# Last modulation loads between the Toeplitz transfers, and the head norm's root on ScalarE

## What is computed

```python
cond = jax.nn.silu(c)
mod = cond @ ada_w[i] + ada_b[i]
h = modulate(rms_norm(x, norm_g[i, 0]), sh_t, sc_t)
...
# S5: diagonal state per group, chunked scan
y = y + d_skip * u32
z = jax.nn.gelu(y)
val, gate = jnp.split(z @ w_glu, 2, axis=-1)
...
# attention, per head and block of 128 queries
p = jax.nn.softmax(jnp.where(mask, s, -jnp.inf), axis=-1)
attn = p[:, :, 0] - lam * p[:, :, 1]
o = attn @ v
o = rms_norm(o, subln_g) * (1.0 - lambda_init)      # over the 128 channels of a head
return o.reshape(bsz, seq_len, d) @ w_o
```

## Time and profile before

| | |
|---|---|
| median of 3 runs | 1313.02 us (1311.71 to 1313.73) |
| the profiled execution | 1311.49 us |
| its span in the trace | 1309.7 us |
| PE busy | 1232.2 us, 94% |
| DVE, ACT, POOL busy | 59%, 39%, 30% |
| chain that ended last | PE 75%, DVE 10%, issue 3%, ACT 2% |

### The profile page before, as it was taken

One profiled execution on the slowest core, in us unless ns is written; L12 is line 12 of the kernel. 1 busy time (PEld: TensorE's weight loads), 2 busy tenths in 40 slices (PEclk: granted clock), 3 DMA queues, 4 the chain that ended last, 5 costly groups with the idle time before them and its releaser, 6 DMA issues.

```text
span 1309.7 us, 17877 instructions
## 1 busy us (share of the span) xinstructions
PE 1232.2 (94%) x6557; PEld 991.2 (76%) x6557; DVE 779.2 (59%) x1096; ACT 508.8 (39%) x780; POOL 393.4 (30%) x267
## 2 busy tenths in 40 slices
PE   4978999899999999999999989898999999999995
PEld 2756888688888887888787767576788888878883
DVE  8976687878954443253955687867754444442323
ACT  3373443243433443132332545445344444442311
POOL 4970100255634342000204343400243344440001
PEclk9988999899989999999999999999899999999997
DMA  7857645146732223231223313111032222223311
GB/s 298 353 161 205 256 165 213 58 165 218 299 136 96 78 99 112 97 127 67 77 97 97 97 50 96 49 65 65 33 102 95 97 97 97 98 97 120 111 51 64
DMA packets 26697, 162.21 MB, mean 124 GB/s; under 512 B 4496, under 2 KB 4816, under 8 KB 8400
## 3 DMA queue, kind: packets, MB, share of 16 engines
q1 hardware_dynamic: 25632, 161.15, 35.0%
q10 hardware_dynamic: 1008, 0.28, 0.1%
HBM read 152.76 MB, written 2.10 MB: 118 GB/s over the span
## 4 chain that ended last, share of the span: by engine, by line
PE 75%; DVE 10%; issue 3%; ACT 2%; POOL 0%; DVEq 0%; ACTq 0%
PE psum L1777 16%; PE psum L1779 16%; PE psum L1778 16%; PE psum L1900 6%; PE psum L1902 6%; PE psum L1901 6%; PE psum L1980 1%; PE psum L1955 1%; PE psum L1940 1%; PE psum L1942 1%; PE psum L1941 1%; DVE wlo L1206 1%; DVE stat L1486 1%; PE psum L1826 1%; DVE ssum L1300 1%
## 5 line engine op out<-in xcount | busy, mean ns | idle before, releaser
L1777 PE MATMUL psum<-hhi,whi 128*128 128x512 f32 x960 | 382.4, 398 | 2.3 <-DVE hlo L1349 1.4
L1779 PE MATMUL psum<-hhi,wlo 128*128 128x512 f32 x960 | 376.3, 392 | 0.0
L1778 PE MATMUL psum<-hlo,whi 128*128 128x512 f32 x960 | 376.2, 392 | 0.0
L1206 DVE TENSOR_TENSOR wlo<-raw,whi 128x2048 fp32r<-128x2048 f32 x81 | 192.4, 2375 | 177.2 <-ACT whi L702 177.2
L544 POOL TENSOR_TENSOR ca<-ca,cb 128x512 f32<-128x512 f32 x44 | 146.2, 3323 | 243.4 <-ACT ca L813 243.4
L702 ACT ACTIVATE whi<-raw 128x2048 fp32r<-128x2048 f32 x80 | 153.2, 1915 | 164.4 <-PE psum L1902 146.1
L1777 PEld LDWEIGHTS psum<-hhi,whi 128*128 128x128 f32 x960 | 181.7, 189 | 43.1 <-issue 2.4
L1779 PEld LDWEIGHTS psum<-hhi,wlo 128*128 128x128 f32 x960 | 181.5, 189 | 38.9
L1778 PEld LDWEIGHTS psum<-hlo,whi 128*128 128x128 f32 x960 | 181.9, 189 | 36.1
L1377 DVE SCALAR_TENSOR_TENSOR ca<-psum,convp,ca 128x511 f32<-128x511 f32 x44 | 33.0, 750 | 219.2 <-ACT ca L809 219.2
L1900 PE MATMUL psum<-ghi,whi 128*128 128x512 f32 x352 | 137.2, 390 | 1.5 <-DVE wlo L1206 1.5
(11 more groups left out here) (334 smaller groups left out, 1676.2 us busy)
## 6 DMA issues: line engine op xcount, KB each, us to landing
raw<-in_units SPq DMA_DIRECT2D x92, 1024.0 KB, 4.8
ada_raw<-in_ada_w SPq DMA_DIRECT2D x24, 1024.0 KB, 7.3
ada_ring<-in_ada_w SPq DMA_DIRECT2D x24, 1024.0 KB, 4.8
qk_sw<-ca SPq DMA_DIRECT2D x32, 128.0 KB, 2.3
u<-in_x_blocks SPq DMA_DIRECT2D x1, 2048.0 KB, 7.6
x<-in_x_t SPq DMA_DIRECT2D x1, 2048.0 KB, 8.5
out_t<-x SPq DMA_DIRECT2D x8, 256.0 KB, 2.0
bc_par<-in_s_bc SPq DMA_DIRECT2D x1, 1024.0 KB, 5.2
```

The source lines that it names most:

```text
L1206: TT(wlo[:, s, :], raw[:, s, :], whi[:, s, :].bitcast(F32), ALU.subtract).then_inc(split_lo, 1)
L1777: M(out, w_hi, hi[:, k, :], start=(k == 0), stop=False)
L1778: M(out, w_hi, lo[:, k, :], start=False, stop=False)
L1779: return M(out, w_lo, hi[:, k, :], start=False, stop=(k == KT - 1))
```

## The change

Three things move in the S5 stage. SP issues modulation loads 21 to 23 between the copies of Toeplitz piece 0 and those of piece 1. PE does `inputs(2)` after modulation unit 18 in place of 19, units 19 and 20 before `local(0)`, and `back(0)` before `local(1)`. ACT copies the second modulation row right after the scaling of piece 1, ahead of half of piece 2's scaling and of the copies of the kernel.

In attention DVE no longer makes the first guess. It signals the variance (`hn_arg`), ACT computes exp(-0.5 ln v) in `head_root` (`Ln`, then `Exp`, on 4 elements a partition) after `turned(a_, 0)` and ahead of the half split of the next weights, and DVE waits for it (`hn_root`) and does one Newton round in place of three. `HEAD_STEPS` counts DVE's linked operations, 5 in place of 13.

```diff
-            for piece in range(2):
-                load_toeplitz(piece)
+            load_toeplitz(0)
             for n in range(21, N_ADA_PE):
                 load_ada0(n)
+            load_toeplitz(1)
             sp.wait_ge(ada_used, N_ADA_PE)
...
             for quarter in range(4):
                 scaled(1, quarter)
+            copy_row(1)
             for quarter in range(2):
                 scaled(2, quarter)
...
-            copy_row(1)
...
+            def head_root(h):
+
+                ln, root = nwt[:, 0, 0:QT], nwt[:, 3, 0:QT]
+                act.wait_ge(hn_arg, h + 1)
+                A(ln, nwt[:, 2, 0:QT], ACT.Ln).then_inc(hn_root, 1)
+                act.wait_ge(hn_root, 2 * h + 1)
+                A(root, ln, ACT.Exp, scale=-0.5).then_inc(hn_root, 1)
...
                 turned(a_, 0)
+                if not first:
+                    head_root(a_ - 1)
...
             copy_output(HEADS - 1)
+            head_root(HEADS - 1)
...
-                lk(TS(t.bitcast(I32), v.bitcast(I32), 1, None, ALU.logical_shift_right))
-                lk(TS(d.bitcast(I32), t.bitcast(I32), -1.0, RSQRT_MAGIC, ALU.mult, ALU.add))
+                dve.sem_inc(hn_arg, 1)
                 yield
-                for i in range(3):
-                    lk(TT(t, d, d, ALU.mult))
-                    lk(STT(t, t, -0.5, v, ALU.mult, ALU.mult))
-                    lk(STT(d, t, 1.5, d, ALU.add, ALU.mult))
-                    if i == 0:
-                        yield
+                dve.wait_ge(hn_root, 2 * h + 2)
+                lk(TT(t, d, d, ALU.mult))
+                lk(STT(t, t, -0.5, v, ALU.mult, ALU.mult))
+                lk(STT(d, t, 1.5, d, ALU.add, ALU.mult))
+                yield
...
             inputs(1)
-            ada_units(16, 20)
+            ada_units(16, 19)
             inputs(2)
+            ada_units(19, 21)
             local(0)
             carried(0)
-            ada_units(20, N_ADA_PE)
+            ada_units(21, N_ADA_PE)
             inputs(3)
+            back(0)
             local(1)
-            back(0)
             carried(1)
```

More of the change, by code:

```diff
@@ L72 @@
 ROUND = 1.5 * 2.0 ** 23
-HEAD_STEPS = 13
+HEAD_STEPS = 5
 RSQRT_MAGIC = float(0x5F3759DF)
@@ L266, in build @@
         mask_ready = sem("mask_ready")
+        hn_arg, hn_root = sem("hn_arg"), sem("hn_root")
         att_step, smax, hn_step = sem("att_step"), sem("smax"), sem("hn_step")
```

## The result

The change takes 1303.69 us, median of five executions (1298.67 to 1304.31), against 1312.94 of the kernel before (1311.71 to 1313.73): ratio 0.9924, 95% interval 0.9905 to 0.9943. That is 9.2 us faster where 16.2 were forecast. The profiled execution took 1303.19 us.

A forecast was written before the change was run, and what follows sets the result against it. The prediction took PE as the bound, gaining only where it waits or runs at the low clock. S5's 6.1 us and attention's 10.1 made 16.2 less, 1295.3 profiled, 1296.8 as median, forecast 1297 us, range 1292 to 1305.

The forecast's parts named there:

- half of attention given back: Rival in attention: semaphore waits use ACT's 0.15 us slack, slow head keeps low clock; attention gives 5 us: 1302; chance 15%.
- both together: Rival: attention gives 5 us and S5, its transfers only reordered, 2.6 us: 1305.5; chance 4%.
- Steps 1 and 2: S5: second row copied early removes 0.72 us wait, worth 0 alone; units 19 and 20 (1.8 us) fill the 3.17 wait.
- Step 3 failed in its size: S5: loads 21 to 23 follow piece 0 on SP; unit 23 starts at 104.15 and ends at 105.1 us.
- Step 4 was right for piece 1: S5: piece 1, copied behind the loads at 131 GB/s, is off at 106.6 to 108.3; local(1) waits at most 0.5 us.
- Step 5 was the right chain: S5: weight units issued at 105.2 instead of 112.20; piece 2 lands at 116.8, 6.4 us earlier; PE waits 2 to 3.
- Step 7's half chance: S5: half a chance that the new wait brings the low clock to local(2), 1.4 us, so 0.7 counted.
- Step 2 held: Steady head: ACT's two loads, Ln and Exp take 2.98 us; exps(2) starts at 778.75; the 0.58 us wait goes.
- The rival in which ACT becomes the bound: Rival: ACT drains between functions, 2.98 us more a head; attention loses 10.4: 1317; chance 6%.
- Step 3 failed: Steady head: DVE's second softmax block 1.2 us earlier, later steps meet PE; 1.65 us in each of four heads: 6.6.
- Step 4: Head at 838 to 856 (second from end): att 2.8 us earlier, weigh 2.3, clock 1.2; together 3.5 us.
- Step 5: First head, last head and tail: ACT costs 0.3 and 0.2, earlier final att gives 0.8, cover just gone; together 0.

## Why the prediction was right or wrong

The sign was right, and 1303.7 lies in the range of 1292 to 1305, but not in the likeliest case (1293.5 to 1299.5). It lies between two rivals, half of attention given back (1302) and both together (1305.5). Attention came out near the first (4.2, where it had 5), but not by what that rival gave as its reason, ACT's slack: the agreement in time is luck. The range held because its upper end was set to take in each of the two halves; both parts of the sum were too large.

**S5.** Forecast 6.1 us; 2.6 at the first GEMM, 3.2 at attention, with 1.1 lost ahead of the stage, where the kernel products ended later, half of it behind an idle time of 2.02 us (1.47 before) that the trace puts down to issue. So the stage itself gave some 4. By the whole time, the S5 part alone gave 5.6.
- Steps 1 and 2 held: no wait for the row, and two units in 1.90 us inside the wait for piece 0, of which 1.57 are left.
- Step 3 failed in its size. Unit 23 was to start 9.85 us after piece 0 was off the engines, as it had after piece 1. It started at 106.01, 1.9 later than forecast: 1.1 of that because piece 0 itself was off the engines only at about 95.4 (94.3 before), and 0.75 because it came 10.6 us after that and not 9.85. The step took the loads as having the engines to themselves; piece 1's copies were issued 0.04 us behind them and ran beside them. The unit then took 1.88 us at the low clock, and not 0.9: the prediction had the low clock cost something only at `local(2)`, and this microsecond stands on the chain that releases the weight units.
- Step 4 was right for piece 1: it had left the engines by 107, and `local(1)` waited for nothing. But its 131 GB/s was no rate of the small copies. In windows of half a microsecond of before nothing moves from 100.0 to 100.5, and then 262 GB/s, which by the order of the queue is the first load. That 106.6 came out is luck in this term.
- Step 5 was the right chain. From the weight units' issue to piece 2 it took 11.5 us (107.95 to 119.47), against 11.0 before. The start was 2.75 us later than the 105.2 forecast (1.1 by piece 0, 0.75 by the loads, the rest by unit 23), and so was the piece (119.47 where 116.8 was forecast). The wait of 2.34 us is in the 2 to 3 forecast.
- Step 6 held, the 0.45 us wait is gone. Step 7's half chance went against it: 1.66 us of low clock in `local(2)`. It was a chance indeed: with the round moved the same place kept the high clock behind a longer wait.
- The experiments add which edit it was: SP's order alone gives all of it, PE's none. Steps 1 and 2, and the order of `back(0)`, are worth nothing that can be measured.

**Attention.** Forecast 10.1 us, got 4.2. The steady heads fell short (2.1 us of 6.6), and not the second head from the end (3.1 of 3.5).
- Step 1 held: no wait at the second block in the steady head.
- Step 2 held almost to the tenth, the tight place included: load, `Ln`, load, `Exp` in 2.98 us, half split 1.04, exponentials at once, and no wait of PE for them. The rival in which ACT becomes the bound was wrong. Without the loads the time is the same within the measurement.
- Step 3 failed: "DVE's second softmax block is still 1.2 us earlier than before". It was 0.16 earlier (9.65 us behind the second block's maximum, 9.81 before). The prediction kept the slow durations of two operations of the block, but let the half split and the round move to an earlier place at the durations of their old place. That place lies beside POOL's sums. The rows of before had held the warning: the two integer operations took 1.22 and 1.19 us for 4 elements where the fastest took 0.17. The prediction read this as a price of those operations, and took it to go with them. It is the price of the place, and goes to whatever stands there: the run without POOL's sums and the one with the round moved show it. With the round behind the fourth maximum the period came to 20.2 us, as the step had said (20.1).
- Step 4: the waits fell from 4.57 us (0.32, 2.98 and 1.27) to 2.16 (0.32, 0.52 and 1.32), and the granted clock rose from 0.81 to 0.91 in a stretch of 18 us. PE's wait for `att` is 2.46 us shorter, near the forecast, but the one for `att_t`, which was to come 2.3 us earlier, is as long as it was. The head took 3.1 us less all the same, clock included.
- Step 5: the final `att` did come earlier, but PE gained 0.26 us by it and not 0.8. The same turn waits for ACT's `cb` too, the copy of what PE turned just before, and that copy now comes last. Before, and after:

```profile
875.16 0.66 PE L1971 MATMUL psum<-ident,att 128*128 128x128 f32 x4 [1.13 <-DVE att L1501]
```

```profile
867.53 0.63 PE L1982 MATMUL psum<-ident,att 128*128 128x128 f32 x4 [0.87 <-ACT cb L873]
```

  The table loads have no part in it: ACT stood idle for 1.46 us ahead of `cb` in both kernels, waiting for PE. The two heads ahead of the steady ones together lost 0.7 us, where 0.3 was forecast for one of them. The tail came out as said, with the cover just gone: the norm's last step ends at 875.47 and PE's turn stands at 875.53.

The Trainium skill (SBUF — State Buffer, Who interferes with whom) states that a VectorE instruction with two inputs in SBUF contends with a GpSimd instruction that reads SBUF, that one in a 2-port mode contends with GpSimd as well, that the shared ports are an exclusive lock, and that the order of issue decides who blocks. The traces agree: 0.16 against 1.23 us for the same 4 elements. No run here shows the ports themselves. They also show the other side. POOL's sums over the run (ns, min/median/max):

```profile
L579 POOL TENSOR_TENSOR qk<-qk,qk_sw x16: 1263/1335/2272, 699.7 to 839.7; 128x512 f32<-128x512 f32 x16
```

One takes 1.26 us at least, and up to 2.27 in a pair that DVE's half split runs beside. In the steady head this can be read as turns, an estimate from these durations: POOL's first sum to about 777.0, DVE's half split (1.2 us of work) to 778.1, POOL's second to 779.23, and the round's first operation behind it, to 779.25.

The Trainium skill (ScalarE: Activation LUTs, What ACT_TABLE_LOAD costs) adds some 1380 ns of drain to every switch to another set. None of the 16 loads here shows it: in the rows above the next activation starts 0.02 us behind the load. The trace decides.

## What to carry to other kernels

When a tiny operation is slow in a trace and fast elsewhere, find what runs beside it before counting its time as saved: the next operation may inherit the place. On a queue of transfers, moving what releases the next issue forward was worth more here (6.1 us) than filling the wait in front of it (nothing measurable); but loads and small copies issued back to back run at once, so the last load landed some 0.75 us later than forecast for loads alone. A copy's rate is read from a window in which nothing else moves. And a gain in an early stage is only the program's once the places with a low clock further on have been read too.

## What the runs showed of the hardware

- A VectorE operation with two inputs of 4 elements a partition takes 0.16 us, and 1.2 where GpSimd sums 128x512 beside it; one such sum takes 1.26 us at least and up to 2.27 beside VectorE's half split, which itself goes from 1.23 to 2.02.
- Two table loads with a small activation behind each take 2.98 us, without a gap, in each of 8 heads; without the 16 loads the program's median was lower by 1.3 us, within the intervals.
- Executions of one kernel on one chip spread by up to 7.3 us (1305.24 to 1312.50 in ten executions, the head norm's part alone). The low clock over 225 to 245 us comes in every profile, but stays for longer in some (granted 0.91 to 0.74); over 620 to 640 us it comes in some and not in others (0.83 to 1.00). From the first GEMM to attention PE took 571.4 us where it was granted 0.74 and 0.83, and 568.3 where it was granted 0.91 and 1.00.
